# The up projection's weights: another landing place, another order, and the norm weight moved into the rows

## The reference

```
def rmsnorm(x, w):
    x32 = x.astype(jnp.float32)
    y = x32 * lax.rsqrt(jnp.mean(jnp.square(x32), axis=-1, keepdims=True) + EPS)
    return y.astype(x.dtype) * w
...
    h = h + rmsnorm(mix, norm_mix_post[layer])
    f = jnp.square(jax.nn.relu(rmsnorm(h, norm_mlp_pre[layer]) @ w_mlp_up[layer])) @ w_mlp_down[layer]
    h = h + rmsnorm(f, norm_mlp_post[layer])
```

## Time and profile before

| | us |
|---|---|
| median of 3 runs | 1623.66 (1622.62 to 1626.65) |
| profiled execution | 1622.92 |
| its span, first to last instruction | 1621.1 |
| TensorE busy | 1550.1 |
| VectorE, GpSimd, ScalarE busy | 1037.5, 823.3, 683.0 |

### The profile page before, as it was taken

How to read it: one execution, slowest core, us unless ns; L and a number is a source line. 1 busy time by engine, 2 the same in 40 slices (tenths; PEclk the granted TensorE clock), 3 DMA queues, 4 the chain that set the end, 5 groups by cost and what they waited for, 6 DMA issues and landing times.

```text
span 1621.1 us, 22591 instructions
## 1 busy us (share of the span) xinstructions
PE 1550.1 (96%) x7951; PEld 1327.4 (82%) x7951; DVE 1037.5 (64%) x1617; ACT 683.0 (42%) x1329; POOL 823.3 (51%) x746
## 2 busy tenths in 40 slices
PE   9999999999999999999999987899888999999997
PEld 8999998878888887888888866777767778888886
DVE  5757434267676768677787767445544568847677
ACT  5322212254444445566654424333333355444443
POOL 7533462156676559643314147766676405505653
PEclk9999999999999999999999988999999999999999
DMA  6455422245656455989886414344333498545666
GB/s 209 108 151 144 131 66 65 66 135 152 180 156 178 131 160 156 328 305 322 296 318 230 159 57 139 114 130 137 130 111 123 151 351 283 195 124 188 194 193 158
DMA packets 225794, 280.63 MB, mean 173 GB/s; under 512 B 21400, under 2 KB 148224, under 8 KB 225696
## 3 DMA queue, kind: packets, MB, share of 16 engines
q1 hardware_dynamic: 224688, 275.69, 52.7%
q0 software_dynamic: 1008, 3.67, 1.2%
HBM read 180.63 MB, written 98.66 MB: 172 GB/s over the span
## 4 chain that ended last, share of the span: by engine, by line
PE 67%; POOL 11%; DVE 9%; DMA 6%; ACT 3%; issue 3%; SPq 1%; DVEq 0%; POOLq 0%; ACTq 0%
PE ps L2935 19%; PE ps L825 7%; PE ps L884 6%; POOL rS L2644 4%; PE ps L2798 4%; PE ps L1799 3%; DMA rA<-w_mlp_up 3%; POOL rA L2640 3%; PE ps L2874 2%; PE ps L1785 2%; PE ps L1768 2%; PE ps L840 2%; PE ps L856 2%; PE ps L1716 2%; PE ps L1738 2%
## 5 line engine op out<-in xcount | busy, mean ns | idle before, releaser
L2935 PE MATMUL ps<-dw_hi,df_hi 128*128 128x512 f32 x448 | 175.1, 391 | 5.0 <-DVE dw_lo L3601 5.0
L2935 PE MATMUL ps<-dw_hi,df_lo 128*128 128x512 f32 x448 | 175.0, 391 | 0.0
L2935 PE MATMUL ps<-dw_lo,df_hi 128*128 128x512 f32 x448 | 174.9, 390 | 0.0
L178 POOL TENSOR_TENSOR ring<-stage,zero 128x512 fp32r<-128x512 f32 (+2 forms) x75 | 83.7, 1116 | 151.5 <-DMA stage<-w_in 48.2
L3596 DVE TENSOR_TENSOR df_lo<-df_raw,df_hi 128x512 fp32r<-128x512 f32 x112 | 120.6, 1077 | 46.4 <-ACT df_hi L3235 46.1
L2935 PEld LDWEIGHTS ps<-dw_hi,df_hi 128*128 128x128 f32 x448 | 84.5, 189 | 23.3 <-issue 3.8
L180 POOL TENSOR_TENSOR ring<-stage,ring 128x512 fp32r<-128x512 f32 (+2 forms) x75 | 100.6, 1341 | 5.9
L3601 DVE TENSOR_TENSOR dw_lo<-dw_raw,dw_hi 128x512 fp32r<-128x512 f32 x96 | 78.8, 821 | 37.9 <-ACT dw_hi L3244 21.5
L3235 ACT ACTIVATE df_hi<-df_raw 128x512 fp32r<-128x512 f32 x112 | 70.2, 627 | 75.5 <-DMA df_raw<-d_f 75.4
L2935 PEld LDWEIGHTS ps<-dw_hi,df_lo 128*128 128x128 f32 x448 | 84.4, 188 | 17.7
L2935 PEld LDWEIGHTS ps<-dw_lo,df_hi 128*128 128x128 f32 x448 | 84.5, 189 | 17.4
(11 more groups left out here) (532 smaller groups left out, 4611.2 us busy)
## 6 DMA issues: line engine op xcount, KB each, us to landing
df_raw<-d_f SPq DMA_DIRECT2D x112, 256.0 KB, 2.7
d_f<-fa SPq DMA_DIRECT2D x105, 256.0 KB, 2.2
dw_raw<-w_mlp_down SPq DMA_DIRECT2D x96, 256.0 KB, 3.0
rA<-w_mlp_up SPq DMA_DIRECT2D x42, 256.0 KB, 3.2
stage<-w_in SPq DMA_DIRECT2D x40, 256.0 KB, 2.7
stage<-w_out SPq DMA_DIRECT2D x28, 256.0 KB, 4.2
xt<-x SPq DMA_DIRECT2D x8, 512.0 KB, 7.2
d_xT<-xdT SPq DMA_DIRECT2D x8, 512.0 KB, 3.3
```

Of the source, the lines that this page charges most:

```text
L178: pool.tensor_tensor(hi, src, k.zero[:, 0:1].broadcast_to([P, width]), ALU.add).then_inc(k.sem(fam + "_hi"), 1)
L2935: mm = pe.matmul(ps[:, base + t, :], F_AT[q % SLOTS][a][:, P * t:P * t + P], W_AT[q % SLOTS][b][:, :], start=(fresh and (a, b) == (0, 0)), ...
```

## The change

1. The norm weight goes into the rows. SyncE writes it once from its column layout to memory (`d_norm`), and loads it back as a row in all partitions (`m_nrow`). VectorE's `normed` replaces ScalarE's `scaled` and multiplies h by the reciprocal root and by that row in one instruction. All multiplications of up weights by the norm weight go: on GpSimd in the early cuts and in the steps (4 of 12 instructions per step), on ScalarE and VectorE in their cuts as a factor.
2. From step 1 on the four quarters land in four tiles of their own (`landing`), one set for all steps, and are read there. A set of weight tiles now has raw values of the sums alone.
3. SyncE issues a step's loads together, ahead of the step's stores: A21 and A11 once GpSimd has made the low part of A11, A22 and A12 once VectorE has made that of A12.
4. Order: ScalarE takes the last row tiles ahead of any weights, and spreads the high parts between the kept copies, all ahead of the relus; VectorE makes its three low parts first and both additions ahead of the first square; one table step stands earlier; GpSimd makes S1 and S2 of step 1 ahead of the first result sums and waits less for the middle; its clearing of semaphores moves to step 4.

The diff, cut:

```
-              {q: o_acc + 4096 * i for i, q in enumerate(("A11", "A12", "S1", "S2", "S3", "S4", "A22"))})
+              {"S1": o_mats1, "S2": o_mats1 + 4096, "A11": o_mats1 + 8192, "A12": o_mats1 + 12288, "S3": o_mats1 + 16384,
+               "S4": O_FB + 6144, "A22": O_FB + 10240})
+    landing = {q: plain(f"land{q}", [P, 4, P], o_landing + 2048 * i) for i, q in enumerate(QUARTERS)}
...
-    HIGHS = ("A11", "S1", "S2", "S3", "A12", "S4", "A22")
+    HIGHS = ("A22", "S1", "A11", "S2", "S3", "A12", "S4")
+    RAW_NEED = {"A22": 1, "S1": 1, "A11": 1, "S2": 2, "S3": 3, "A12": 4, "S4": 4}
+    def unsplit(i, q):
+        return sums[i % 2][q] if q[0] == "S" else first_in[q] if i == 0 else landing[q]
...
+        sp.dma_start(k.d_norm.rearrange("(k p) -> p k", p=P), k.par[:, PARAM["mlp"]:PARAM["mlp"] + KD], allow_slow_non_contiguous=True).then_inc(sem("e_w_in"), 16)
...
+        sp.wait_ge(sem("s_sent"), 32 * NT)
+        sp.wait_ge(sem("e_w_in"), 16)
+        sp.dma_start(nrow[:, :], k.d_norm.partition_broadcast(P)).then_inc(sem("e_w_in"), 16)
...
-            if more:
-                load_quarter(i + 2, "S3")
+            if i + 2 < STEPS:
+                sp.wait_ge(sem("x_plo"), 4 * (i + 1) + 1)
+                load_quarter(i + 2, "A21")
+                load_quarter(i + 2, "A11")
+                sp.wait_ge(sem("x_dlo"), 3 * (i + 1) + 3)
+                load_quarter(i + 2, "A22")
+                load_quarter(i + 2, "A12")
...
-        def weights(i):
...
-            pool.wait_ge(sem(f"x_q{i % 2}"), 64 * (i // 2) + 64)
-            scaled("S3")
-            scaled("A22")
...
+        def weights_begun(i):
+            own = sem("x_raw")
+            if i:
+                pool.wait_ge(sem("x_q1"), 64 * i)
...
+            if i >= 2:
+                pool.wait_ge(sem("v_up"), UP + 7 * (i - 1))
+            pool.tensor_tensor(sums[i % 2]["S1"][:, :, :], unsplit(i, "A21")[:, :, :], unsplit(i, "A22")[:, :, :], ALU.add).then_inc(own, 1)
+            pool.wait_ge(own, 4 * i + 1)
+            pool.tensor_tensor(sums[i % 2]["S2"][:, :, :], sums[i % 2]["S1"][:, :, :], unsplit(i, "A11")[:, :, :], ALU.subtract).then_inc(own, 1)
+        def weights_ended(i):
+            own = sem("x_raw")
+            if i == 1:
+                pool.wait_ge(sem("v_up"), UP)
+                pool.wait_ge(sem("f_sent1"), 16 * len(F_KEPT))
...
+        weights_begun(0)
+        weights_ended(0)
+        weights_begun(1)
         first_sums(fb, 6, 0)
         first_sums(fa, 8, 4)
+        weights_ended(1)
...
+            more = i + 1 < STEPS
             if i:
-                for n in range(3):
-                    kept(i, n)
-            if i + 1 < STEPS:
-                weights_high(i + 1, HIGHS[:4])
-            relu(i, 0)
...
+                kept(i, 0)
+            if more:
+                weights_high(i + 1, "A22", "S1", "A11")
+            if i:
+                kept(i, 1)
...
+        def normed(t):
+            i = stat[2, t]
+            dve.wait_ge(sem("m_rs"), 5 * i + 5)
...
+            dve.scalar_tensor_tensor(hn[:, t % 2, :], h[:, t % 2, :], r[:, i:i + 1], nrow[:, :], ALU.mult, ALU.mult).then_inc(sem("m_hn"), 1)
...
+            if more:
+                weight_low(i + 1, "A22")
+                weight_low(i + 1, "S3")
+                weight_low(i + 1, "A12")
             total(i, 0)
+            total(i, 1)
             squared(i, 0)
```

More of the change, by code:

```diff
@@ L2474, in load_quarter @@
         def load_quarter(i, q):
-            e, half_k = {"A11": (0, 0), "A12": (0, 1), "S3": (1, 0), "A22": (1, 1)}[q]
-            if i >= 2:
-                sp.wait_ge(sem("v_up"), UP + 7 * (i - 2) + PRODUCTS.index(q) + 1)
-            sp.dma_start(raws[i % 2][q][:, :, :], up_q[FIRST_SUB + i, e, half_k]).then_inc(sem(f"x_q{i % 2}"), 16)
+            e, half_k = QUARTERS[q]
+            sp.dma_start(unsplit(i, q)[:, :, :], up_q[FIRST_SUB + i, e, half_k]).then_inc(sem("x_q1" if i else "x_q0"), 16)
         def store_tile(g, q, src):
@@ L2512, in on_sync @@
         sp.wait_ge(sem("m_mm"), len(UNITS))
-        load_quarter(0, "S3")
+        load_quarter(0, "A21")
         load_quarter(0, "A12")
+        for u in range(2):
+            sp.wait_ge(sem(f"m_sent{u}"), 16 * NT // 2)
+        sp.wait_ge(sem("m_hn"), NT)
+        for q in ("A21", "A22", "A11", "A12"):
+            load_quarter(1, q)
         store_first(0, 6)
         store_sums(1, 0)
-        sp.wait_ge(sem("v_up"), UP)
-        for u in range(2):
-            sp.wait_ge(sem(f"m_sent{u}"), 16 * NT // 2)
-        for q in ("S3", "A22", "A11", "A12"):
-            load_quarter(1, q)
         store_first(6, 8)
@@ L2526, in on_sync @@
             done = UP + 4 * i
-            more = i + 2 < STEPS
-            if more:
-                load_quarter(i + 2, "A11")
             if i == STEPS - 1:
@@ L2549, in on_sync @@
             store_tile(g, "S1", ftile("S1"))
-            if more:
-                load_quarter(i + 2, "A12")
             sp.wait_ge(sem("v_sq"), done + 3)
@@ L2556, in on_sync @@
                 store_tile(g, q, ftile(q))
-            if more:
-                load_quarter(i + 2, "A22")
             sp.wait_ge(sem("v_sq"), done + 4)
@@ L3219, in on_scalar @@
         for i in range(STEPS):
+            more = i + 1 < STEPS
             if i:
-                for n in range(3):
-                    kept(i, n)
-            if i + 1 < STEPS:
-                weights_high(i + 1, HIGHS[:4])
-            relu(i, 0)
-            if i + 1 < STEPS:
-                weights_high(i + 1, HIGHS[4:])
-            for n in range(1, 4):
+                kept(i, 0)
[4 more added lines that the diff above has]
+            if more:
+                weights_high(i + 1, "S2", "S3")
+            if i:
+                kept(i, 2)
+            if more:
+                weights_high(i + 1, "A12", "S4")
+            for n in range(4):
                 relu(i, n)
@@ L3506, in up_sub @@
             summed_tile(i, 2)
-            if more:
-                weight_low(i + 1, "A22")
             squared(i, 3)
@@ L3538, in on_vector @@
         stats(2, 0)
+        normed(0)
         fused(1)
@@ L3567, in on_vector @@
         low_tile(NT - 1)
+        dve.wait_ge(sem("m_lo"), 2 * NT)
+        table_step(1)
         first_square(3)
-        dve.wait_ge(sem("m_lo"), 2 * NT)
-        table_step(0)
-        table_step(1)
-        for q in ("S3", "A12", "A22"):
+        table_step(2)
+        for q in ("A22", "S3", "A12"):
             weight_low(0, q)
-        table_step(2)
+        table_step(3)
         first_square(4)
-        table_step(3)
         table_step(4)
+        table_step(5)
         first_square(5)
-        table_step(5)
         table_step(6)
```

125 lines of the change are left out of this document (60 added, 65 removed).

## The result

The changed kernel takes 1581.53 us (median; 1578.84 to 1583.48), the kernel before took 1624.64 on the same chip (1622.62 to 1626.65): a ratio of 0.9734, 95% interval 0.9713 to 0.9754. The forecast was 1563, with a range from 1555 to 1577. The direction was right, the size was not: 18.5 us of the expected gain are missing.

What follows compares the result with a forecast made beforehand. TensorE is busy 96% of the span, so only idle time and low-clock stretches can be had. Terms -45.4 - 10.9 - 5.6 + 1.5 = -60.4 us from 1622.92 give 1562.5, as median 1563 us; range 1555 to 1577.

Steps and rivals of the forecast that it cites:

- Steps 1 to 13: Up stage, steps 1 to 13: no wait of TensorE late in a step, steps run dense at 19.04 us, -45.4 us.
- The timetable: Within each of steps 1 to 13: due times of sums, high parts, low parts and additions; A22 has 1.9 us of cover.
- queued in the wrong place: Up-stage steps: the second addition, which frees A22, stands behind a square and a low part; it could have run at S3's end.
- a ring over stores and loads: Up-stage steps: the last quarter's load stands behind the previous step's stores, GpSimd starts 7.65 us in, and each step repeats it.
- isn't short of data in any other way: Up-stage steps: apart from the addition queued in the wrong place, TensorE lacks no data; no size of its own.
- The banks: Last banks of the plain product: the 8.09 us wait before bank 4 goes, with the low clock after it, -10.9 us.
- Step 0: First up-stage step: VectorE is the bound, stalls before S1, S2 and A22; 26.1 us instead of 31.66, -5.6 us.
- the low clock: Step 0: 1.5 us of slower matmuls, counted behind the 2.3 us stall at A22.
- The middle: Where rows are normalised: eight row scalings become VectorE instructions of 1.28 us, most vanish in gaps, +1.5 us.
- The rival in which all eight normalisations are on the path: Middle: VectorE bounds it, the eight cost up to 10.2 us, 1572, or 1576 with a late table chain; chance 0.13.
- The new transfers: Norm weight's store in 4-byte pieces and its load back: 0 us, bounds up to +5 for the store, +2 for the load.
- The down stage: Down stage: new places of some tiles cost nothing and the order stays, 0 us.

## Why the prediction was right or wrong

**Steps 1 to 13: right, to 0.8 us.** The timetable held. Step 7 starts at 1125.71. VectorE's low parts were forecast about 4, 7.3 and 9.5 us into the step, the additions at 10.9 and 13.6:

```profile
1129.78 1.52 DVE L3488 TENSOR_TENSOR wA_0lo<-landA,wA_0hi 128x512 fp32r<-128x512 f32 x1 [1.43 <-ACT wA_0hi L3188]
1133.03 1.23 DVE L3488 TENSOR_TENSOR wS_0lo<-rS,wS_0hi 128x512 fp32r<-128x512 f32 x1 [1.72 <-ACT wS_0hi L3188]
1135.22 0.74 DVE L3488 TENSOR_TENSOR wA_0lo<-landA,wA_0hi 128x512 fp32r<-128x512 f32 x1 [0.97 <-ACT wA_0hi L3188]
1136.86 0.70 DVE L3495 TENSOR_TENSOR ps<-ps,f_kept 128x512 f32<-128x512 f32 x1 [0.90 <-PE ps L2944]
1139.58 0.70 DVE L3495 TENSOR_TENSOR ps<-ps,f_kept 128x512 f32<-128x512 f32 x1 [2.02 <-PE ps L2944]
```

They come 4.1, 7.3 and 9.5, 11.15 and 13.9 us into it. The loads are issued in two pairs, from 8.0 and from 10.3 us into the step (forecast 7 and 11.3), early enough.

**The cause named for those steps: half wrong.** The prediction gave two, "queued in the wrong place" for the addition and a ring over stores and loads, and said that TensorE "isn't short of data in any other way". The first fell: with the additions in the right place alone the time didn't change. The second was shown from both sides: one load moved gives 38 to 39 us, the loads moved back take 38 to 40 away. With the load moved, the second addition still stands behind the first square and a low part, and in steps 1 to 13 TensorE waits for it 4.7 us in all, in place of 29.2: it was late because GpSimd's late start had made the whole queue late. The right sum for these steps thus rests on a cause of which only the second half holds; the timetable had both in it, so the number alone could not tell. (A small misreading beside it: by the earlier trace rows product S3 ends at 1158.45, 60 intervals of 0.2266 us behind 1144.85, not at 1158.2.)

**The banks: the wait and its size right (-10.4), the gain not all kept.** The last row tile came in time, as worked out. That the time behind it stays gained is another claim, and in the kernel before it doesn't hold: with the tile's order alone the time is 1621.48 against 1622.51.

**Step 0: wrong by 9.1 us, the step of the sum that failed.** The prediction took "2.35 us a step, 3.64 for one that runs beside GpSimd", had the last table step done at 966.7 and a stall of 1.8 before S1. It was done at 982.9, and the stall was 7.8. Of these 16.2 us, 8.8 are the later start of everything (bank 4 at 953.63 rather than 943.34 + 1.5), which moves TensorE too and makes no stall. The rest is that the higher duration was used for one step of the chain, though the text itself had GpSimd beside the chain, and had quoted the 0.68 against 1.78 us of the earlier trace rows. The seven table steps from 951.32 on took 24.35 us (3.52, 3.76, 4.54, 2.85, 2.35, 3.44 and 3.89); by the prediction's durations they are 6 x 2.35 + 3.64 = 17.7. These 6.6 us more, and the three weight low parts among them (1.78 each, about 0.65 before), cover the 6.0 by which the stall before S1 was put too small. Most of what is left of the 9.1 is a second term that was sized too small: the low clock. The prediction counted 1.5 us of it, behind A22 alone, and its terms (19.04 + 1.8 + 1 + 2.3 + 1.5) add up to 25.6, not 26.1; measured are 5.1. The rule of the Trainium skill ("SBUF — State Buffer", who interferes with whom) that two such instructions exclude each other was weighed for the middle, where it cost little; it belonged here, and the durations of this stretch agree with it. With GpSimd's eight result sums shrunk, step 0 takes 25.9 us; the forecast had 26.1 with all of that work done. The waits were in the places forecast (S1 and A22; none came before S2); the second, 3.2 for 2.3, was near in size, but its cause was VectorE's queue, in which the additions stand behind three low parts with no gap between them, as the version with the additions first shows, and not late weights of GpSimd's.

**The middle: +1.5 forecast, +2.4 to +3.4 measured** (the four kernels with the direct load). The rival in which all eight normalisations are on the path didn't come: the eight instructions ran at 1.28 us, and one wait of 2.26 us stands behind the first. Its premise was misread: between 872.69 and 884.13 VectorE is not without a gap, it waits 1.22 and 1.05 us there for ScalarE's squares (at 875.45 and 881.82 in the trace of before), where part of the new instruction finds room.

**The new transfers: 0 forecast, about +5 measured.** This step failed as well. The store was priced by when its data is wanted, and bounded at +5 by the landing time of another transfer; what it cost was the time of the transfers behind it on SyncE's queue. Alone it costs 5.2 (ratio) to 6.2 us (medians); taken out of the changed kernel, with the row loaded from the input instead, it gives back 6.3 to 7.1. The intervals of these ratios, 0.001 to 0.002 wide on either side, don't tell the two apart, and by the start of bank 0 they are 5.2 and 5.3. The rest of the +10.2 ahead of bank 0 is the middle's, and some 2 to 3 us are the profiled execution's own.

**The down stage: 0 forecast, no difference measured.** The +1.5 of the table lies within what this stretch scatters by from one profiled kernel to the next (319.3 to 323.2 us).

## What to carry to other kernels

The last wait in a loop names the instruction that came last, not the one that is late. Before you price it, move that instruction alone, or follow the loop once around to the transfer that starts each pass. Where two engines that slow each other both work through a stretch, use the durations of the rows in which they meet for all of it, not for one instruction: here, changing the order within such a stretch only moved the wait (twice), and less work for one of the two shortened it. And price a transfer of many small pieces by what stands behind it, not by when its data is needed.

## What the runs showed of the hardware that was not expected

- A store of 1024 pieces of 4 bytes from 128 partitions to memory took 15.0 to 16.8 us to land. From 13 to 14 us behind it on, six issues on SyncE took 1.0 to 3.7 us each; four of them took 0.3 to 0.5 before. It cost the kernel 5.2 us, though its own data was wanted by nobody.
- Where VectorE and GpSimd meet, both pay: 2.35 becomes up to 4.54 us for a pair of VectorE's table steps, 1.3 becomes 2.2 to 2.3 for a sum on GpSimd.
- The low clock behind idle time adds to each loss: in step 0 of the changed kernel 11.0 us without work come with 5.1 us of slower matmuls (24.1 busy for 19.04).
